# Expert matrices of a mixture-of-experts stage, loaded with each partition's rows contiguous in DRAM

## The reference, cut to what matters

```python
def expert_choice_ffn(h, router_w, w1, w3, w2):
    ...
    aff = jax.nn.softmax(jnp.dot(xf, router_w).astype(jnp.float32), axis=-1)
    gate, idx = lax.top_k(aff.T, cap)
    xe = xf[idx]
    hid = jax.nn.silu(jnp.einsum('ecd,edf->ecf', xe, w1)) * jnp.einsum('ecd,edf->ecf', xe, w3)
    ye = jnp.einsum('ecf,efd->ecd', hid, w2) * gate[..., None].astype(h.dtype)
    out = jnp.zeros_like(xf).at[idx.reshape(-1)].add(ye.reshape(-1, D).astype(xf.dtype))
```

## Time and profile before

| what | us |
|---|---|
| executions of the kernel before | 1924.89, 1927.45, 1928.77 (median 1927.45) |
| the profiled execution, its own time | 1921.78 |
| its span, first to last instruction | 1919.7 |
| mean granted TensorE clock in it | 0.928 of full speed |

### The profile page before, as it was taken

One profiled execution on the slowest core, in us unless ns is written; L12 is line 12 of the kernel. 1 busy time (PEld: TensorE's weight loads), 2 busy tenths in 40 slices (PEclk: granted clock), 3 DMA queues, 4 the chain that ended last, 5 costly groups with the idle time before them and its releaser, 6 DMA issues.

```text
span 1919.7 us, 37494 instructions
## 1 busy us (share of the span) xinstructions
PE 1578.0 (82%) x16252; PEld 1038.2 (54%) x16252; DVE 680.6 (35%) x1357; ACT 461.7 (24%) x818; POOL 203.6 (11%) x202
## 2 busy tenths in 40 slices
PE   5999967779769999878999775877777948989893
PEld 2544324445346666643655454777664526766662
DVE  5135574541520000122151498444552171100003
ACT  4111474440311111112100355322211032111110
POOL 0000000000011111100000000444440001111103
PEclk8999988989879999989999897999888979999997
DMA  9612462443369999971221000000003018999994
GB/s 343 238 44 87 175 230 88 166 153 120 143 239 365 368 369 365 374 237 39 88 91 44 1 1 1 2 2 2 2 2 143 1 55 305 357 372 368 369 377 150
DMA packets 147564, 330.02 MB, mean 172 GB/s; under 512 B 10613, under 2 KB 16361, under 8 KB 147465
## 3 DMA queue, kind: packets, MB, share of 16 engines
q1 hardware_dynamic: 133264, 287.29, 41.1%
q0 software_dynamic: 9168, 32.65, 6.3%
q10 hardware_dynamic: 5032, 8.65, 1.3%
HBM read 303.79 MB, written 24.78 MB: 171 GB/s over the span
## 4 chain that ended last, share of the span: by engine, by line
PE 57%; DMA 17%; DVE 15%; issue 6%; ACT 5%; SPq 1%; ACTq 0%; DVEq 0%; POOL 0%
PE pairs L191 25%; DMA arena<-in_exp_w 15%; PE pairs L1254 10%; PE pairs L1270 4%; DVE sm L1600 1%; PE pairs L1895 1%; PE pairs L1666 1%; PE pairs L952 1%; PE pairs L1897 1%; ACT arena L1535 1%; PE pairs L1076 1%; PE pairs L563 1%; DVE sm L876 1%; DVE arena L2132 1%; PE pairs L1927 1%
## 5 line engine op out<-in xcount | busy, mean ns | idle before, releaser
L191 PE MATMUL pairs<-hT,ring 128*128 128x128 f32 (+1 forms) x1120 | 305.2, 435 | 2.1 <-ACT hT L310 2.1
L191 PEld LDWEIGHTS pairs<-hT,ring 128*128 128x128 f32 x1120 | 170.0, 192 | 137.4 <-issue 136.0
L310 ACT ACTIVATE arena<-pairs 128x256 f32<-128x256 f32 (+7 forms) x188 | 120.5, 655 | 494.5 <-PE pairs L191 259.3
L191 PE MATMUL pairs<-ring,hT 128*128 128x512 f32 (+1 forms) x448 | 176.8, 556 | 0.0
L1254 PE MATMUL pairs<-arena 128*64 128x80 f32 x4096 | 152.9, 238 | 26.8 <-DMA arena<-in_exp_w 21.1
L1254 PEld LDWEIGHTS pairs<-arena 128*64 128x64 f32 x4096 | 149.5, 141 | 40.8 <-issue 38.7
L1254 PEld LDWEIGHTS pairs<-arena,ring 128*64 128x64 f32 x4096 | 143.0, 137 | 29.6 <-issue 29.6
L1254 PE MATMUL pairs<-arena,ring 128*64 128x80 f32 x4096 | 145.7, 233 | 15.9 <-DMA ring<-in_exp_w 13.9
L1323 DVE TENSOR_TENSOR arena<-hT,pairs 128x80 f32<-128x80 f32 x128 | 30.5, 238 | 293.5 <-ACT hT L1299 293.5
L191 PEld LDWEIGHTS pairs<-ring,hT 128*128 128x128 f32 x448 | 85.0, 190 | 90.6 <-issue 87.5
L1327 DVE TENSOR_SCALAR hT<-pairs,arena 80x512 f32<-80x512 f32 x32 | 23.9, 747 | 256.1 <-ACT hT L1304 256.1
(11 more groups left out here) (374 smaller groups left out, 2149.2 us busy)
## 6 DMA issues: line engine op xcount, KB each, us to landing
arena<-in_exp_w SPq DMA_DIRECT2D x48, 2048.0 KB, 21.2
ring<-in_exp_w SPq DMA_DIRECT2D x48, 2048.0 KB, 21.4
ring<-in_w_mod SPq DMA_DIRECT2D x24, 2048.0 KB, 7.9
ring<-in_w_in_ab SPq DMA_DIRECT2D x5, 2048.0 KB, 8.1
ring<-in_w_in_cd SPq DMA_DIRECT2D x5, 2048.0 KB, 7.8
ring<-in_w_out SPq DMA_DIRECT2D x4, 2048.0 KB, 8.1
moe_rows<-arena POOLq DMA_DIRECT2D x2, 2560.0 KB, 14.6
h_rows<-arena POOLq DMA_DIRECT2D x2, 2560.0 KB, 8.4
```

Of the source, the lines that this page charges most:

```text
L191: last = pe.matmul(out, lhs(k), rhs(k), start=(k == 0), stop=(k == KD - 1))
L310: return eng.activation(dst, src, ACT.Copy) if eng is nc.scalar else eng.tensor_copy(dst, src)
```

## The change

The views of the three matrices now put rows `8p` to `8p + 7` of w1 and w3, and rows `4p` to `4p + 3` of w2, on partition `p`: 16 KiB that follow each other in DRAM, for all three. The load is written as one run of 4096 elements per partition.

The rest follows from that. The token rows' transposes take every eighth column of `xe`, so that block `k` of `xeT` holds the elements `8p + k` (weights with a step of 8 elements, 32 bytes). Since w2's partition `p`, block `f`, now is hidden column `4p + f`, the first products take every fourth column of w1 and w3 (weights with a step of 4 elements, 16 bytes) in place of 64 adjacent ones. The number and the shapes of all instructions stay. Waits, the order of loads, the second product and all of the other loads stay as they are.

```diff
-        W1 = [io["exp_w1"][l].rearrange("e (k p) f -> p (e k) f", p=P) for l in range(2)]
-        W3 = [io["exp_w3"][l].rearrange("e (k p) f -> p (e k) f", p=P) for l in range(2)]
-        W2 = [io["exp_w2"][l].rearrange("e (k p) d -> p (e k) d", p=P) for l in range(2)]
+        W1 = [io["exp_w1"][l].rearrange("e (p k) f -> p e (k f)", p=P) for l in range(2)]
+        W3 = [io["exp_w3"][l].rearrange("e (p k) f -> p e (k f)", p=P) for l in range(2)]
+        W2 = [io["exp_w2"][l].rearrange("e (p k) d -> p e (k d)", p=P) for l in range(2)]
...
-                    last = pe.transpose(ps[:, o:o + CAP], xe[par][:, k * P:k * P + P], ident[0:CAP, 0:CAP])
+                    last = pe.transpose(ps[:, o:o + CAP], xe[par][:, k::KD], ident[0:CAP, 0:CAP])
...
-                w1, w3 = (slots[s + j].rearrange("p (k n) -> p k n", n=FF) for j in range(2))
+                w1, w3 = (slots[s + j].rearrange("p (k q f) -> p k f q", f=FT, k=KD) for j in range(2))
...
-                                last = pe.matmul(ps[c:c + 64, o:o + CAP], w[:, k, f * P + c:f * P + c + 64], rhs,
+                                last = pe.matmul(ps[c:c + 64, o:o + CAP], w[:, k, f, c:c + 64], rhs,
...
-            kk = FT if j == 2 else KD
-            n = D if j == 2 else FF
-            src = w[:, bass.ds(i * kk, kk), :]
-            sp.dma_start(slots[s].rearrange("p (k n) -> p k n", n=n), src).then_inc(w_here[s], 16)
+            sp.dma_start(slots[s].unsqueeze(1), w[:, bass.ds(i, 1), :]).then_inc(w_here[s], 16)
```

## The result

The changed kernel takes **2090.37 us** (median of 4, 2089.36 to 2095.81) where the one before takes 1926.78 (4 runs, 1924.89 to 1928.77): ratio 1.0855, 95% interval 1.0833 to 1.0877, 163.6 us slower. The profiled execution took 2095.81 us, with a span of 2093.6.

The account below looks back on a forecast made before the run. DMA loads were taken to bound both expert stages, 18.85 us per expert against PE's 16.57. Savings of 15 + 14 = 29 us took the profiled 1921.8 us to 1893, a median of about 1898; range 1889 to 1915.

Parts of the forecast that it names:

- What bounds the kernel: Bulk of both expert stages: bound by DMA loads at 18.85 us per expert, against PE's own pace of 16.57.
- The loads' gain: Expert matrix loads in longer runs: 15 us saved in the first layer and 14 in the second, 29 us.
- w2's 0.20 us per expert: w2's loads, going from 4 KiB to 16 KiB runs: 2.439 to 2.345 us per MB, 0.20 us per expert.
- w1's and w3's 0.92 us: w1's and w3's loads, going from 2 KiB to 16 KiB runs: 2.564 to 2.345 us per MB, 0.92 per expert.
- The fit: Load time split into per-byte and per-packet parts from 390 and 410 GB/s, giving 426 GB/s for 16 KiB runs.
- the price of the first products' weight reads: Every-fourth-column weight loads in first products: taken as nothing; bounded above by doubled reading, 4.6 us per expert.
- rival A: PE becomes the bound, first products' weights read at half rate: 21.4 us per expert, 2037 us; chance 0.20.
- The free 17 ns: First products: a pair of halves takes 70.4 ns and reading 53, so 17 ns per pair were held free.
- The upper bound: First products' weight loads: reading at most twice as slow, 53 to 106 ns per 64 columns.
- The transposes: Token rows' transposes with stepped weight loads: 0.2 to 0.3 us more per expert, hidden in waiting, taken as nothing.
- GpSimd's queue: GpSimd's 4 KiB packets beside 16 KiB ones: gathers may land later than 7.3 us, but a few us are covered.
- The threshold: First products: the kernel gets slower than before only from 9 ns more per product (2.3 us / 256).

Follow-up runs that it names:

- e1: Kernel before, with only w1 and w3 in 16 KiB runs and transposes on every eighth column; w2 and first products unchanged: 1903.78 us, ratio 0.9875.
- e3: Changed kernel with its 16 KiB loads kept, but transposes and first products reading adjacent columns (computes another sum): 1904.01 us, ratio 0.9877 to the kernel before.
- e4: Kernel before, with w2 in two 8 KiB runs per partition, so first products read every second column: 1925.76 us, ratio 0.9994.
- e10: Changed kernel with first products not split in halves, 128 weight columns per product: 2596.42 us in one execution.
- e5: Kernel before, with first products' weight columns at steps 2, 3, 8 and 4 in the four column blocks (another sum): 2000.74 us in one execution.
- e9: Kernel before, with an expert's eight transposes reading columns at steps 1, 2, 3 and 4, two each (another sum): 1921.84 us in one execution.
- e8: Kernel before, with w1 and w3 in 16 KiB runs and token columns permuted in ScalarE's PSUM copies, so transposes read adjacent columns: 1903.52 us, ratio 0.9888.
- e2: Kernel before, with only w2 in 16 KiB runs, so first products read every fourth column; w1, w3 and transposes unchanged: 2080.20 us, ratio 1.0802.
- e6: Kernel before, with adjacent weights but moving token columns at steps 2, 3, 4 and 1 in the four column blocks (another sum): 1995.53 us, one execution.
- e11: Changed kernel with first products split in quarters, 32 weight columns per product, 512 products per expert: 2222.48 us, ratio 1.1558.

## Why the prediction was wrong

**What bounds the kernel** was read rightly: the loads, at 18.85 us per expert, with PE at 16.57 close beneath. e1 and e3 show that the loads bound it, since longer runs alone bring the time down.

**The loads' gain** had the right sign and was somewhat too large. 29 us were forecast; e3 has 23 (interval 20 to 27) and e1 24. Where the loads bind, an expert takes 18.1 us in e1 and 18.2 in e3 (the starts of the first products of six experts, 669.2 to 778.3 us) where 17.7 was worked out: 0.7 us less than before in place of 1.1. Two terms are too large by that. w2's 0.20 us per expert, 5 us in all, doesn't show in e3 against e1 nor in e4 against before, though neither pair is close enough to exclude it; and w1's and w3's 0.92 us measured 0.7. That 29 less 5 gives the 24 us measured looks like a coincidence: in the profiled executions e1's two stages are 9.6 and 8.4 us shorter than before, 18 in all and not 24. The fit was made on loads that ran alone. In the stage the rate rose from 368 to 384 and 383 GB/s while the DMA share fell from 1.04 to 1.02 and 1.01; at a share of 1.04 these rates would be 392 and 394, near the 390 that the text named. So longer packets seem to overlap less and to lose part of their gain by that; no run tests it. (The range has a slip of its own: 1927 - 36 is 1891, and not 1889.)

**The step that failed** is the price of the first products' weight reads: "I take nothing, because 17 ns per pair are free today". The text's own sign for rival A, L1254 x256 above 10 us with a DMA share under 1.0, is what came: 15.52 us and 0.83. The free 17 ns were not enough, by far: a pair of halves takes 121 ns, so 51 ns more than its 70.4. The argument under it, that a float32 weight load uses each column twice and so leaves the reader time for a new place per 0.83 ns, is refuted by the rows of 217 and 330 ns: 1.77 ns per column in place of 0.83 (e10), with 104 ns of the load outside the reading (217 - 64 x 1.77). With the same 104 ns taken off, 128 columns of a transpose with a step take 102 to 117 ns and 128 of a product 226, twice as much. So it looks as if the float32 weight load reads each column twice, both times at the slow price, rather than reading it once and using it twice; this is an inference from these figures. The upper bound failed too, since twice the reading (53 to 106 ns) is not the worst: the reading of 64 columns is 113 ns by these rows, and a pair of halves takes 121, so up to 2.3 times the 53. The nearest rows could not bound it, because no row of before reads with a step; a factor of two was my choice and stood in the text as if it were an end. So rival A, the one that came true and had 0.20, was priced at 2037 us, 53 us short of 2090: its period was put at 21.4 us and is 23.43. The 2.0 us between them lie in the products (15.52 against 9.01 + 4.6 = 13.6) and the transposes (0.34 more against 0.2 more). The 3 us that it added to each stage don't show: 16 x 23.43 is 374.9, and a stage is 374.1 us long.

The rule of the Trainium skill that the text set against the change (page "SBUF — State Buffer", section "Door 1: The DMA port swizzle": 16-byte lines, full rate from two hits in a line on) is what e4 and e5 show for the first products: two columns in a line cost 0 to 2 ns per product, one costs 25. For a transpose's weight load it doesn't hold in this form: two hits in each line, at step 2, cost as much as one (216 and 221 ns, e9).

**The transposes** were bounded at 0.2 to 0.3 us and cost 0.34. The text's own figures give even less, (107 - 88) x 8 = 0.15 us; and its 0.42 ns per column of a transpose is 0.44 when the 84 ns that a weight load takes beside its reading (137 - 53) are taken off the 140. That this would be hidden while the loads bind, and appear otherwise, came out in both directions: nothing in e1 and e8, 10 us between e2 and the changed kernel.

**GpSimd's queue** behaved as said. A gather takes 9.9 us to land in the changed kernel where it took 7.3, and nobody waits for it. The view of that line in the changed kernel:

```profile
DMA to landing us min/median/max: 4.1/9.9/11.0
```

**The threshold** of 9 ns more per product, named as the point at which the kernel turns slower, was not tested closely. The runs only enclose it: 0 to 2 ns more in e4 left the time as it was, 15 ns more on average in e5 and e6 (12.9 and 12.8 us for 256 products) gave 2000.74 and 1995.53 us, and the changed kernel's 25 are far beyond. The result needed no more than this one number, which no view of the kernel before has.

## What to carry to other kernels

A layout that makes DRAM runs longer must be followed to the engine that reads the tile: for float32 on TensorE, columns two apart in a product's operands were almost free here, columns four or eight apart made its weight load more than twice as long to read, and moving columns four apart doubled a product's time. A transpose's weight load paid in full from two apart. Split such a change by matrix: here w1 and w3 could have their long runs with only a hidden step in the transposes (1904 us), and w2's were worth nothing that could be measured and cost 187 us (2090.4 - 1903.8). Where the trace has no row for an access pattern, the upper end of its price is unknown rather than "twice", and the chance of the other side should follow from how little slack there is (9 ns per product), not from an argument about how the reader might work.

## What the runs showed of the hardware that was not expected

- A float32 weight load of a product, 64 columns: 137 ns adjacent, 138 at step 2, 174 at step 3, 217 at steps 4 and 8. Per column that is 0.83 ns adjacent (137 and 190 ns at 64 and 128 columns) and 1.77 at step 4 (217 and 330). A transpose's, 128 columns: 140 ns adjacent, 206 to 221 at steps 2, 3, 4 and 8.
- Column groups of the array are read side by side: with step 4, 128 columns take 233 ns in one load, 121 in two halves, 77 in four quarters while instructions last and the clock is full.
- With twice the code in the expert loop TensorE stood still after 128 or 255 products, 229 us in all; the instruction queue's packets went from 76 to 218 (e11).
- In e10 PE was busy without a gap and still the granted clock fell to a mean of 0.63 of full speed, a mix of its levels of 1.2 and 2.4 GHz, with the weight loads long and the products few (623 in 160 us). The second products show it, 7.85 us in the rows above in place of 6.87. The weight loads don't: 330 ns each and 233 ns from product to product at either level. What bounds them is not TensorE's clock.
- ScalarE's copies out of PSUM with a step of 8 elements cost nothing (e8).
